# A two-block transformer kernel whose operand tiles are moved 32 bytes in SBUF

## What is computed

```python
for i in range(2):                                  # first block
    u = rmsnorm(h, norm_g[i]) @ w_in[i]             # 2048 -> 5632
    a_val, a_glu, a_z, q, k, v, b_z = split(u)
    ya = conformer_conv(a_val, a_glu, ...) * silu(a_z)
    yb = window_attention(q, k, v, bias, sink[i]) * silu(b_z)
    h = h + concatenate([ya, yb]) @ w_out[i]        # 2048 -> 2048
    e = rmsnorm(p[i] @ w_pe[i], pe_g[i])            # 256 -> 2048
    h = h + e * sigmoid(h @ w_pg[i])                # 2048 -> 2048
...
x = x + (fox_attention(...) * silu(gate)) @ fox_w_out   # fox_w_in: 2048 -> 8224
x = x + (swa_attention(...) * silu(gate)) @ swa_w_out   # swa_w_in: 2048 -> 4608
return rmsnorm(x, final_g_2)
```

## Time and profile before

| | |
|---|---|
| median of 3 runs | 1758.4 us |
| lowest and highest | 1757.22 and 1760.55 us |
| the profiled execution's own time | 1758.62 us |
| its span | 1756.8 us |
| TensorE busy | 1737.4 us (99%), 14,389 matmuls |
| VectorE busy | 1307.2 us (74%) |
| ScalarE busy | 904.0 us (51%) |
| mean of HBM traffic over the span | 184 GB/s |
| mean granted TensorE clock | 0.999 |

### The profile page before, as it was taken

One profiled execution on the slowest core, in us unless ns is written; L12 is line 12 of the kernel. 1 busy time (PEld: TensorE's weight loads), 2 busy tenths in 40 slices (PEclk: granted clock), 3 DMA queues, 4 the chain that ended last, 5 costly groups with the idle time before them and its releaser, 6 DMA issues.

```text
span 1756.8 us, 35798 instructions
## 1 busy us (share of the span) xinstructions
PE 1737.4 (99%) x14389; PEld 1668.2 (95%) x14389; DVE 1307.2 (74%) x2087; ACT 904.0 (51%) x1326; POOL 38.9 (2%) x48
## 2 busy tenths in 40 slices
PE   8999999999999999999999999999999999999998
PEld 7999999999999999999999898998989999999986
DVE  7999899977779987998776764656555666677655
ACT  5433665555544465546465463545455553665553
POOL 0000000000000000000000110000100000000000
PEclk9999999999999999999999999999999999999999
DMA  7676655555666665556556666655655556555564
GB/s 235 192 216 186 192 149 175 194 192 194 197 185 216 197 200 145 156 185 205 187 193 188 205 196 189 194 183 165 215 166 181 192 180 180 164 168 166 171 196 136
DMA packets 200092, 326.21 MB, mean 186 GB/s; under 512 B 14912, under 2 KB 66320, under 8 KB 199822
## 3 DMA queue, kind: packets, MB, share of 16 engines
q1 hardware_dynamic: 197085, 320.85, 58.5%
q10 hardware_dynamic: 2864, 3.36, 0.6%
HBM read 320.42 MB, written 2.69 MB: 184 GB/s over the span
## 4 chain that ended last, share of the span: by engine, by line
PE 90%; DVE 6%; ACT 1%; issue 1%; SPq 1%; DMA 1%; POOL 0%; ACTq 0%; DVEq 0%; POOLq 0%
PE g L495 70%; PE g L504 11%; DVE w_lo L917 2%; PE att L614 2%; PE att L659 2%; PE att L638 2%; DVE cacc L1163 1%; ACT w_hi L1546 1%; DVE u L1042 1%; ACT u L1555 0%; PE att L566 0%; SPq L308 0%; PE att L495 0%; DMA stage<-in_w_in_dram 0%; PE g L525 0%
## 5 line engine op out<-in xcount | busy, mean ns | idle before, releaser
L917 DVE TENSOR_TENSOR w_lo<-stage,w_hi 128x1024 fp32r<-128x1024 f32 x577 | 704.1, 1228 | 368.5 <-ACT w_hi L1546 367.7
L1546 ACT CAST w_hi<-stage 128x1024 fp32r<-128x1024 f32 x577 | 602.2, 1054 | 619.0 <-PE g L495 418.0
L495 PE MATMUL g<-a_hi,w_hi 128*128 128x256 f32 x2496 | 699.2, 280 | 1.2 <-DVE a_lo L1097 1.0
L495 PE MATMUL g<-a_lo,w_hi 128*128 128x256 f32 x2496 | 691.1, 277 | 0.0
L495 PE MATMUL g<-a_hi,w_lo 128*128 128x256 f32 x2496 | 691.1, 277 | 0.0
L495 PEld LDWEIGHTS g<-a_hi,w_hi 128*128 128x128 f32 x2496 | 469.9, 188 | 8.8 <-issue 7.3
L495 PEld LDWEIGHTS g<-a_lo,w_hi 128*128 128x128 f32 x2496 | 469.1, 188 | 0.0
L495 PEld LDWEIGHTS g<-a_hi,w_lo 128*128 128x128 f32 x2496 | 468.9, 188 | 0.2
L495 PE MATMUL g<-b_hi,w_hi 128*128 128x256 f32 x1440 | 401.1, 279 | 0.0
L495 PE MATMUL g<-b_hi,w_lo 128*128 128x256 f32 x1440 | 398.4, 277 | 0.0
L495 PE MATMUL g<-b_lo,w_hi 128*128 128x256 f32 x1440 | 398.4, 277 | 0.0
(11 more groups left out here) (232 smaller groups left out, 1387.1 us busy)
## 6 DMA issues: line engine op xcount, KB each, us to landing
stage<-in_fox_w_in_dram SPq DMA_DIRECT2D x128, 512.0 KB, 4.2
stage<-in_w_in_dram SPq DMA_DIRECT2D x112, 512.0 KB, 3.8
stage<-in_swa_w_in_dram SPq DMA_DIRECT2D x72, 512.0 KB, 3.9
stage<-in_w_in_dram SPq DMA_DIRECT2D x128, 256.0 KB, 3.1
stage<-in_w_out_dram SPq DMA_DIRECT2D x64, 512.0 KB, 4.3
stage<-in_w_pg_dram SPq DMA_DIRECT2D x64, 512.0 KB, 4.1
stage<-in_fox_w_out_dram SPq DMA_DIRECT2D x32, 512.0 KB, 4.3
stage<-in_swa_w_out_dram SPq DMA_DIRECT2D x32, 512.0 KB, 4.4
```

Of the source, the lines that this page charges most:

```text
L495: mm = pe.matmul(acc[:, j * S:(j + 1) * S], w[:, slot, c0 + j * P:c0 + (j + 1) * P], xx[:, k, :], start=st and m == 0 and j % 2 == 0, stop ...
L917: dve.tensor_tensor(w_lo[:, slot, :], stage[:, slot, :], w_hi[:, slot, :].bitcast(F32), ALU.subtract).then_inc(*t.inc("w_split"))
L1546: act.copy(w_hi[:, slot, :], stage[:, slot, :]).then_inc(*t.inc("w_rounded"))
```

## The change

The gap before the operand tiles grows from 240 to 248 words, so from 960 to 992 bytes. All tiles declared behind it, from `a_hi` to the last small one, begin 32 bytes further on; `stage`, `w_hi` and `w_lo` stay where they are. The instructions of every engine, their order and their waits are the same.

```diff
@@ -43,7 +43,7 @@
 NDVE = CC
 CONSTS = 14
 REL = 512
-APART = 240
+APART = 248
 REL0 = S - 1
 CM = 3 * P
 FH = 32
```

## The result

The changed kernel takes 1804.46 us (median of 4 runs, 1803.88 to 1808.58) where the kernel before took 1757.81 us in the same comparison: a ratio of 1.0272, with a 95% interval of 1.0252 to 1.0291. It is 2.7% slower. The forecast had the sign, and its likeliest case, +20 us, was less than half of what came; the first rival, +46 to +56 us, is what happened.

The account below looks back on a forecast made before the run. TensorE's matmul count times start spacing was taken to bound the kernel. The profiled 1758.6 us plus 20 for streamed-weight matmuls, all other terms 0, gave 1778.6, against the median 1778.5 us; range 1749 to 1814.

Parts of the forecast that it names:

- likeliest case: Streamed-weight matmuls: half of all 11,808 at the wide spacing instead of 1,450, +20 us; chance 0.35 for 1765 to 1804 us.
- Rival 1: Streamed-weight matmuls: everything leaves the dense spacing, +46 to +56 us, 1804 to 1815 us; chance 0.17.
- What bounds the kernel: TensorE, busy 1737.4 of 1756.8 us, does not wait for weights; time is matmul count times spacing between starts.
- Loads, splitting, other tiles at 0: Weight loads, cast and subtraction at lines 1546 and 917, VectorE's taps, matmuls between two moved tiles: 0 us.
- The two spacings: Streamed matmuls start 0.1133 or about 0.1178 us apart; a stretch keeps the pattern in which it starts.
- Line 504: Its 720 matmuls with 512 columns, 0.2285 us each: taken as 0, bounds -1.4 to +5.1 us.
- Rival 2: Nine long stretches and short ones behind scores go from 0.1178 to 0.1133: at most 6.5 us faster, 1752 us; chance 0.21.
- The denser pattern: Streamed matmuls at a spacing between 0.109 and 0.1133 us, 1702 to 1745 us; chance 0.07.
- Rival 3: No difference, 1755 to 1762 us: distance does not matter at this grain or leaves the shares as they are; chance 0.20.
- the time that I drew from the rule of SBUF: TensorE's two independent read ports, for moving operand and weight load, mean no effect: 1758.4 us.

Follow-up runs that it names:

- e1: Against the kernel before, a 32-byte pad ahead of stage moves rings and operand tiles alike, gap still 960 bytes; 1761.7 us against 1761.35, ratio 1.000.
- e2: Against the kernel before, a 32-byte pad behind b_lo moves only h, u and all later tiles, gap still 960 bytes; 1764.91 us, ratio 1.0023.

## Why the prediction was right and wrong

**What bounds the kernel: right.** The time is a number of matmuls times their spacing; in all runs TensorE kept 1.00 of its clock in these stretches, and only the spacing moved.

**Loads, splitting, other tiles at 0: right.** `e1` and `e2` show it, and VectorE's taps kept their time, 478 ns in the median instead of the earlier trace rows's 483. `e2`'s 0.2% comes from which pattern the stream is in; whether moving the other tiles favours the wide one, or 8 runs fell that way, stays open, since its interval begins at 1.0003.

**The two spacings, and that an interruption chooses between them: right,** and tested by the dummy turns. It would also explain why the kernel before varies, 21 of its runs between 1754.7 and 1774.2 us, though only one of its executions has a trace. The profiled executions of the kernels at residue 192 speak for it: 8,856 dense matmuls and 1754.8 us with 448 bytes, 8,640 and 1758.6 before, 8,160 and 1762.2 in `e1`, 7,944 and 1764.9 with 192 bytes. In the profiled execution with 192 bytes (1764.94 us, at the top of its runs) the whole stretch from 860 to 930 us is wide, x597, where the kernel before has it dense.

**The step that failed** is the one for the matmuls of the earlier trace rows: "480 is nearer to 448 than to 384, so both patterns should still exist", with half of the matmuls at the wide spacing, +20 us. I had the nearness in bytes stand for nearness in price, and the runs show that it doesn't: 32 bytes on either side lose the dense pattern as completely as 64 do, while at 64 modulo 256, 128 bytes from 192, it exists. The term itself, put at 20 us, measured 49.4; all 10,350 dense matmuls going wide had been priced as the upper case at 46 to 56 us. The evidence that I discounted was the earlier trace rows, the only other distance in the trace. I held against it that those matmuls might have inherited their pattern; with 1024 bytes they are dense directly behind wide ones, so they had not. That still said nothing of 480 itself: it showed that a distance without the dense pattern exists, not that this is one. A move that keeps both patterns and shifts the shares, which is what I forecast, is real, but it is the case of 64 bytes, not of the change.

**Line 504: right within its bounds.** +3.8 us by one stretch, +4.2 by all starts, inside -1.4 to +5.1.

**The rivals.** Rival 1 came true. Rival 2 needs a distance at which the dense pattern exists; of the eight only the old one and 64 have it, and 64 mostly misses it. The denser pattern, down to 0.109 us, showed at no residue. Rival 3 fails by measurement, and so does the time that I drew from the rule of SBUF — State Buffer, section Who interferes with whom, in the Trainium skill, that TensorE never waits for anyone: with every instruction the same, the gap between two tiles moves the time from 1758 to 1822 us. Whether TensorE waits for its own second read, no run shows. Nor do these matmuls reach the 109.2 ns of TensorE: Matmul & The Clock Gate, section Back-to-back issue gap, in the Trainium skill: 113.3 to 120.1 ns are measured. The prediction left out that the section gives this formula as the gap of an isolated matmul and other values for a stream of weight loads and matmuls, so it was no bound for this loop.

**What is shown and what is argued.** Shown: the spacings that the stream can have follow the ring-to-operand distance modulo 256 bytes, not the tiles' own starts, and they are a property of the whole sequence of terms; where there are two, interruptions shift the shares. Argued only: that the read of the next stationary tile and that of the moving tile get in each other's way. No run takes one of the two reads away, so how they collide stays open, and so does why 64 and 192 have the dense pattern and why this kernel finds it at 192 so much more often.

## What to carry to other kernels

When a matmul loop has no idle time and still runs above its column count, compute the spacing between starts by stretch, (length + one duration) / count, and look whether the same loop shows several values; if it does, where the two streamed tiles lie against each other is a term to measure, with all residues of it, since neighbours say nothing about each other. Read the spacing over the whole trace and not in one stretch: from 400 to 470 us the run with 64 bytes shows nothing of its dense pattern. If the trace already holds another value of the quantity that the change moves, as `pe_hi` did here, give what it shows more weight than nearness, though it bounds only its own value. Dummy work that "settles" an engine is tied to the layout: with 992 bytes it only costs its own time.

## What the runs showed of the hardware

Two tiles' distance modulo 256 bytes in a partition changes the spacing of 128x128 by 256 column float32r matmuls between 0.1133 and 0.1200 us, 6%, and the kernel by up to 3.7%. The dense and the widest spacing differ by 0.0067 us, which is 16 cycles at the 2.4 GHz level at which the clock was granted. The same stream can hold either of two spacings for hundreds of matmuls at one layout (0.1133 and 0.1178 us at 192 and at 64, 0.1173 and 0.1187 at 160) and only one at the next (0.1183 at 224).

The 512 column form, in which weights move and operands are stationary, doesn't follow the same order. Line 504 with 1024 bytes:

```profile
1750.00:1780.00 30.00, 30.00 (x134) 24.83 (x133) 1.00 0.61 194
```

(30 + 0.39)/134 = 0.2268 us, 0.0017 less than at the old distance and 0.0070 less than at the changed one, though 0 modulo 256 is among the two worst for line 495. With 720 of them against 11,808 it decides nothing here.
